# Attention by chosen keys: the products without a reader between the first two short tiles are taken out

## The reference, cut to what matters

```
def block_fn(args):                      # one block of 128 queries
    sc = einsum(relu(einsum(iqb, ik) * IDX_DIM**-0.5), iwb)      # a score for each key, from 8 small heads
    sc = where(key_pos <= qpos, sc, -inf)
    _, idx = top_k(sc, 256)                                       # 256 keys for each query
    att = einsum('bqhd,bqkd->bqhk', qb, k[idx]) * HEAD_DIM**-0.5
    probs = softmax(where(idx <= qpos, att, -inf))
    return einsum('bqhk,bqkd->bqhd', probs, v[idx])
out = all blocks * silu(g)
```

## Time and profile before

| what | value |
|---|---|
| median of three executions | 3945.34 us |
| the profiled execution's own time | 3943.82 us |
| its span, first to last instruction | 3942.5 us |
| mean granted clock of TensorE | 0.963 |
| busy: TensorE / VectorE / ScalarE / GpSimd | 3591.7 / 2161.7 / 1149.2 / 484.3 us |
| `dsa_attend`, layer 0 and layer 1 | about 110 and 108 us |

### The profile page before, as it was taken

One profiled execution on the slowest core, in us unless ns is written; L12 is line 12 of the kernel. 1 busy time (PEld: TensorE's weight loads), 2 busy tenths in 40 slices (PEclk: granted clock), 3 DMA queues, 4 the chain that ended last, 5 costly groups with the idle time before them and its releaser, 6 DMA issues. The chain is left out here.

```text
span 3942.5 us, 57710 instructions
## 1 busy us (share of the span) xinstructions
PE 3591.7 (91%) x22944; PEld 2273.9 (58%) x22944; DVE 2161.7 (55%) x4617; ACT 1149.2 (29%) x2489; POOL 484.3 (12%) x304
## 2 busy tenths in 40 slices
PE   7999768899999997999997887998999998888898
PEld 5455434784478544656665775444655665776344
DVE  3243465446764573599865654342389965663333
ACT  2212354220122011411134555222320124555222
POOL 0020023000100010012211111110002221221110
PEclk9999879999999998999998998998999999999899
DMA  7432422324533442123331204111013331202220
GB/s 242 142 107 80 149 78 97 104 97 150 189 103 113 150 171 84 33 64 96 112 110 51 73 22 169 51 61 58 27 48 102 107 139 54 60 31 104 96 81 22
DMA packets 234285, 377.17 MB, mean 96 GB/s; under 512 B 30743, under 2 KB 163871, under 8 KB 233015
## 3 DMA queue, kind: packets, MB, share of 16 engines
q1 hardware_dynamic: 234030, 373.58, 28.7%
HBM read 290.84 MB, written 69.08 MB: 91 GB/s over the span
## 5 line engine op out<-in xcount | busy, mean ns | idle before, releaser
L3442 PE MATMUL win_acc<-across_room,across_hT 128*128 128x384 f32 (+3 forms) x3072 | 908.7, 456 | 3.7 <-PEq L83 3.7
L3442 PEld LDWEIGHTS win_acc<-across_room,across_hT 128*128 128x128 f32 x3072 | 561.5, 191 | 345.4 <-issue 15.4
L2506 DVE TENSOR_SCALAR_CACHE_REDUCE win_over<-d_sc,win_mid 128x384 uint8<-128x384 f32 (+5 forms) x384 | 337.9, 942 | 25.3 <-DVE win_mid L2517 24.5
L3281 PE MATMUL tail_wo<-tail_w_out,across_room 128*128 128x512 f32 x512 | 229.0, 601 | 9.3 <-issue 9.3
L3503 ACT ACTIVATE d_ot<-win_acc 128x384 f32<-128x384 f32 (+1 forms) x144 | 67.3, 468 | 574.9 <-PE win_acc L3442 574.9
L491 PE MATMUL zin_acc<-zin_wt,across_hT 128*128 128x512 f32 (+2 forms) x640 | 229.2, 513 | 0.0
L3292 PE MATMUL tail_wg<-tail_w_gate,across_room 128*128 128x512 f32 x512 | 226.5, 597 | 1.0 <-DVE across_room L3122 1.0
L491 PEld LDWEIGHTS zin_acc<-zin_wt,across_hT 128*128 128x128 f32 x640 | 119.9, 190 | 98.3 <-issue 88.6
L3281 PEld LDWEIGHTS tail_wo<-tail_w_out,across_room 128*128 128x128 f32 x512 | 97.6, 193 | 128.3 <-issue 128.3
L1728 PE MATMUL mlp_bk<-across_hT,across_room 128*128 128x256 f32 x768 | 171.0, 379 | 0.0
L3292 PEld LDWEIGHTS tail_wg<-tail_w_gate,across_room 128*128 128x128 f32 x512 | 96.9, 192 | 117.4 <-issue 117.4
(11 more groups left out here) (495 smaller groups left out, 6606.6 us busy)
## 6 DMA issues: line engine op xcount, KB each, us to landing
across_room<-in_w SPq DMA_DIRECT2D x96, 1024.0 KB, 6.9
across_room<-in_w_in SPq DMA_DIRECT2D x18, 1536.0 KB, 8.8
s_z<-d_ot SPq DMA_DIRECT2D x14, 1536.0 KB, 6.5
across_room<-in_w_ada SPq DMA_DIRECT2D x8, 2048.0 KB
across_hT<-s_z SPq DMA_DIRECT2D x16, 832.0 KB, 5.4
win_zp<-d_ot SPq DMA_DIRECT2D x8, 1344.0 KB
zin_wt<-in_w_in SPq DMA_DIRECT2D x4, 2048.0 KB, 9.4
tail_w_out<-in_w_out SPq DMA_DIRECT2D x4, 2048.0 KB, 10.5
```

Of the source, the lines that this page charges most:

```text
L2506: s.put(dve.tensor_scalar(over[q][:, :], sc[q][:, :], mid[:, q:q + 1], 0.0, ALU.is_gt, ALU.add, accum_out=cnt[:, q:q + 1]))
L3281: mm = pe.matmul(wo[:, c, :], yT[:, n % 2, q, :], W["out"][:, q, c * COL:(c + 1) * COL], start=q == 0, stop=q == KC - 1)
L3442: mm = pe.matmul(acc[:, u % RING, 0:w], hT[:, k, t * P:(t + 1) * P], wt[:, i % 2, k, 0:w], start=k == 0, stop=k == KC - 1)
```

## The change

The function `keep_busy`, the function `busy_after` and their two calls go. The order of all other instructions and all waits stay as they are.

```
@@ dsa_attend, TensorE's program
-                def keep_busy(j, n):
-                    for _ in range(n):
-                        pe.matmul(po[:, j, 256:512], B["v"][:, 0:2, :].rearrange("p b c -> p (b c)"), B["g"][:, 0, :], start=True, stop=True)
-
                 def scores(m):
...
-                def busy_after(m):
-                    i, h = m // DSA_H, m % DSA_H
-                    if i < 2 and h < DSA_H - 1:
-                        keep_busy(i % 2, 8 if m == 2 * DSA_H - 2 else 2)
-
                 scores(0)
                 scores(1)
-                keep_busy(0, 16)
                 k = 0
                 for m in range(NM):
                     if m + 2 < NM:
...
                         turn(k)
                         if k >= 1:
                             values(k - 1)
-                            if groups[k - 1][0] != m:
-                                busy_after(m - 1)
                         k += 1
                 values(k - 1)
```

## The result

The changed kernel takes 4029.71 us (median of four, 4000.81 to 4060.97); the kernel before 3942.03 (four, 3938.71 to 3945.44). A fifth execution of the changed kernel, not in the median, took 3999.03 us. The ratio is 1.0185, 95% interval 1.010 to 1.027: slower, where 16.5 us less had been forecast; whether by more than 2% is open. The profiled execution has a span of 4053.8 us against 3942.5 and a mean granted clock of 0.922 against 0.963.

The account below looks back on a forecast made before the run. VectorE's chain, waiting behind the removed products, was taken to bound the stage's front, TensorE the rest from head 12. Gains of 9.1 + 7.4 = 16.5 us off 3943.82 gave 3927.3, stated as 3928; range 3920 to 3940.

Parts of the forecast that it names:

- (a): Layer 0, VectorE: head 2 starts at about 2011.6 instead of 2016.88, 5.3 us gained of 8.8 us removed.
- (b): Head 2 to the reciprocal of tile 0: 1.2 us come back; reciprocal at 2017.3 with a fast clock.
- the upper bound of 31.5 us: TensorE's own time in the removed products, 16.6 and 14.9 us by layer, gained only if nothing else is in the way.
- (c): Tile 0's reciprocal to head 8, first of tile 7: mostly VectorE's own work; head 8 at 2021.7, against 2028.31.
- The clock's term: From the stage's start until dense scores, TensorE at 1.2 GHz: costs 1.1 us of layer 0's 10.2.
- The first rival: The clock stays low over the dense tiles, from head 12 on and before: up to 60 us a layer; chance 0.08.
- (d): Head 8 to head 10 on VectorE: head 10 starts at 2028.5 to 2029, 11 us earlier than 2039.92.
- (e): At head 12 TensorE becomes the bound: its scores start 10 us earlier; 10.2 us in layer 0 with a fast clock.
- Theory by barrier: From the experiments: idle time at the barrier sets the low clock, and only dense products right after it help.
- by fixed hold: From the experiments: once low, the clock is held low for a fixed time, 195 us.
- by transposes: From the experiments: transposes don't count as work that restores the clock.

Follow-up runs that it names:

- the kernel with the late run: The changed kernel with one run of 16 products of 128 rows by 256 columns put in after head 12; 3980.97 us.
- the kernel with ten products and tile 0's runs: The kernel before with its first run cut from 16 to 10 products and, of the later runs, only tile 0's three runs of two kept; 3925.85 us, ratio 0.9965.
- the one with late 64-row products: The changed kernel with 16 products of 64 rows put in after head 12; 4062.04 us.
- the first-run kernel: The changed kernel with only the first run of 16 products put back, in both layers; 4040.56 us, ratio 1.013.
- the kernel with the later runs: The changed kernel with the five runs of two products and the run of eight put back, first run left out; 3957.67 us, ratio 1.0042.

## Why the prediction was wrong

- *Steps (a) and (b)* held. Head 2 at 2011.55 (said: within 0.3 of 2011.5), the reciprocal at 2018.5 (said: 2017 to 2018.5), at the late end: the 1.2 us that (b) takes back didn't come, as TensorE at 1.2 GHz kept VectorE waiting 2.12 us for 1.99. TensorE's own time, the upper bound of 31.5 us, was tested by no run.
- *Step (c)* was late already: head 8 at 2024.9 with 2.18 us of idle time before it, for 2021.7 to 2023.5. Its four score records took 3.78 us, as the text allowed (3.7); the sum had them start too early.
- *The step that failed is the clock.* "So I take 1.2 GHz from the stage's start until dense scores come": the fall was right (0.54 in the front part), the return was not. The scores of tile 7 are dense in TensorE's busy time, but use 64 rows, and in the profiled execution some 150 us of them, with transposes and short products between, did not restore the clock. The clock's term in the sum was 1.1 us a layer; it cost 58.6 + 10.2 in layer 0 and 60.3 + 8.5 in layer 1, about 69 us each, in that execution, and 51 to 62 us less over both layers in three of the five. The first rival had the mechanism, the place (long tiles), and the price, up to 60 us a layer, at a chance of 0.08. The arguments against it were the failing ones. That the tiles hold 1.00 today says what keeps a clock, not what restores it (the kernel with the late run shows both in one stage). The returns in other stages came with other work: the one of 540 to 550 with products of 128 rows by 512 columns, and the one of 3603 to 3611 after 8 us in which four transposes and four 64-row products took turns (0.50 until 3605, 1.00 from 3606), so that transposes were about half of the time. In the changed kernel's long tiles they are about a fifth: a head of 8.38 us has eight, 1.8 us of it. It was called the same mix and is not; that this difference decides is argued, not tested.
- *The chain behind the clock* (steps (d) and (e); 10.2 us in layer 0 and 8.5 in layer 1 with a fast clock) was right in direction; its size is only in part shown. With 128-row scores, low at the head and back by head 8, the products' leaving moves head 12 by 5.4 us and the two layers by 11.7, of 16.5 forecast. But the pace is another there. With 64-row scores the kernel with ten products and tile 0's runs, which holds back less than before but not nothing, has stages shorter by 8.9 and 5.5 us. No run has 64-row scores, no products and a fast clock.
- *Theory by barrier, by fixed hold and by transposes* fell in the experiments above. Not settled: why the clock comes back inside the long tiles in some executions of the changed kernel, and of the one with late 64-row products; no profile of such an execution was taken, only the one of the first-run kernel, in which it came back in tile 6 in both layers.

## What to carry to other kernels

A product that nobody reads can be holding a clock, not only time: before taking one out, ask whether what is left could raise the clock from 1.2 GHz again, not whether it holds 2.4 GHz. Look for stages of 64-row or short products: they kept a fast clock in these runs and restored a low one late, in some executions, or not at all. Filling the rows with zeros made the real work do the job of the fillers, and was the faster pace as well. Read busy time together with the granted clock: at 0.50 four score records show as 3.35 us busy and at 1.00 as 1.77, which looks like more work and isn't.

## What the runs showed of the hardware that was not expected

Both levels of the clock can last under the same work: 1.00 over 68 us of long tiles in the kernel with the later runs, 0.50 over 118 us of the same tiles in the changed one, TensorE busy 66.42 and 117.01 us of them. The low one is the less sure of the two: in the first-run kernel it ended by itself after 37.6 us in each layer, and no trace here shows a long tile that lost 1.00. Transposes of 128 by 128 restored the clock (64 in 8.60 us), 64-row products (32 records in 14.02 us) and 64-column ones (64 records in 13.86 us) didn't; scores over 128 rows with zeros in 64 of them restored it as those without zeros did. Scores over 128 rows in place of 64 shortened a head from 4.41 to 4.12 us at the same clock, although the products are as long (1.72 and 1.77 us for four records): about 0.14 us of it lie between the start of the scores and that of the transposes behind them (1.70 and 1.56 us), the rest at the starts that follow. That this is the price of changing between 64-row and 128-row work is my reading, not a test.
